# Feed-forward input products with 512 moving columns, and weights laid out in order of use

## What is computed

```python
def conv_glu_ffn(h, w_in, conv_w, conv_b, w_out):
    a, b = jnp.split(h @ w_in, 2, axis=-1)
    taps = conv_w[:, None, :]
    a = lax.conv_general_dilated(a, taps, ...) + conv_b      # depthwise, causal, 3 taps
    return (jax.nn.silu(a) * b) @ w_out

def _swiglu(h, w_in, w_out):
    gate, up = jnp.split(h @ w_in, 2, axis=-1)
    return (jax.nn.silu(gate) * up) @ w_out
```

## Time and profile before

| | |
|---|---|
| median of 3 runs | 2264.7 us |
| the profiled execution | 2262.3 us, its span 2260.5 us |
| TensorE matmuls / weight loads | 2098.9 us (93%) / 1978.4 us (88%), 15863 each |
| DVE, ACT, POOL busy | 1170.3, 981.6, 546.8 us |
| granted TensorE clock | 0.938 of full on average |
| chain that ended last | TensorE 82%, DVE 10%, ACT 5% |
| HBM | 142 GB/s over the span |

### The profile page before, as it was taken

How to read it: one execution, slowest core, us unless ns; L and a number is a source line. 1 busy time by engine, 2 the same in 40 slices (tenths; PEclk the granted TensorE clock), 3 DMA queues, 4 the chain that set the end, 5 groups by cost and what they waited for, 6 DMA issues and landing times.

```text
span 2260.5 us, 36891 instructions
## 1 busy us (share of the span) xinstructions
PE 2098.9 (93%) x15863; PEld 1978.4 (88%) x15863; DVE 1170.3 (52%) x1402; ACT 981.6 (43%) x1144; POOL 546.8 (24%) x153
## 2 busy tenths in 40 slices
PE   6988999969999997999976999999999989899999
PEld 5975799968789997999976899989999989669999
DVE  4335466755556766445786644334444432765433
ACT  3323344443444434434624444357434447544433
POOL 1100012221112231322142122453022256211232
PEclk8966799989999998999988999999999999899999
DMA  9400144535224553555521265535555535523653
GB/s 224 154 25 0 57 149 168 178 124 164 98 96 166 187 191 102 189 184 163 184 94 56 95 204 184 169 117 171 185 164 190 183 125 160 140 65 114 204 168 111
DMA packets 265345, 322.17 MB, mean 143 GB/s; under 512 B 15837, under 2 KB 245076, under 8 KB 264980
## 3 DMA queue, kind: packets, MB, share of 16 engines
q1 hardware_dynamic: 252692, 304.49, 41.1%
q0 software_dynamic: 2816, 9.44, 1.7%
q10 hardware_dynamic: 9728, 6.67, 1.4%
HBM read 319.45 MB, written 1.12 MB: 142 GB/s over the span
## 4 chain that ended last, share of the span: by engine, by line
PE 82%; DVE 10%; ACT 5%; issue 1%; ACTq 1%; DMA 1%; POOL 1%; SPq 0%; DVEq 0%
PE bank L370 23%; PE bank L371 22%; PE bank L372 22%; DVE lo L343 3%; PE bank L411 2%; PE bank L430 2%; ACT hi L337 1%; PE bank L433 1%; PE bank L413 1%; PE bank L446 1%; PE bank L1624 1%; ACT arena L1566 1%; PE bank L1405 1%; DVE arena L1480 1%; DVE xl L754 1%
## 5 line engine op out<-in xcount | busy, mean ns | idle before, releaser
L370 PE MATMUL bank<-xh,hi 128*128 128x256 f32 x3208 | 931.0, 290 | 55.5 <-DVE xl L754 22.9
L371 PE MATMUL bank<-xl,hi 128*128 128x256 f32 x3208 | 917.1, 286 | 0.0
L372 PE MATMUL bank<-xh,lo 128*128 128x256 f32 x3208 | 916.3, 286 | 0.0
L343 POOL TENSOR_TENSOR lo<-ring,hi 128x2048 fp32r<-128x2048 f32 x100 | 472.6, 4729 | 1470.9 <-ACT hi L337 1470.9
L337 ACT ACTIVATE hi<-ring 128x2048 fp32r<-128x2048 f32 x291 | 550.5, 1899 | 482.0 <-PE bank L372 465.3
L343 DVE TENSOR_TENSOR lo<-ring,hi 128x2048 fp32r<-128x2048 f32 (+1 forms) x191 | 502.8, 2633 | 410.7 <-ACT hi L337 410.5
L370 PEld LDWEIGHTS bank<-xh,hi 128*128 128x128 f32 x3208 | 624.7, 195 | 69.3 <-issue 38.1
L371 PEld LDWEIGHTS bank<-xl,hi 128*128 128x128 f32 x3208 | 625.0, 195 | 4.9 <-issue 4.8
L372 PEld LDWEIGHTS bank<-xh,lo 128*128 128x128 f32 x3208 | 624.6, 195 | 0.2
L370 PE MATMUL bank<-gg,hi 128*128 128x256 f32 x1056 | 303.9, 288 | 20.2 <-DVE gg L695 20.2
L371 PE MATMUL bank<-gg,hi 128*128 128x256 f32 x1056 | 303.1, 287 | 0.0
(11 more groups left out here) (234 smaller groups left out, 2041.9 us busy)
## 6 DMA issues: line engine op xcount, KB each, us to landing
ring<-in_ffn_w_in SPq DMA_DIRECT2D x132, 1024.0 KB, 5.1
ring<-in_ffn_w_out SPq DMA_DIRECT2D x66, 1024.0 KB, 4.9
ring<-in_w_kv SPq DMA_DIRECT2D x24, 1024.0 KB, 5.2
ring<-in_a_w_in SPq DMA_DIRECT2D x16, 1024.0 KB, 5.5
ring<-in_od_w_in SPq DMA_DIRECT2D x12, 1024.0 KB, 6.5
ring<-in_b_w_q SPq DMA_DIRECT2D x12, 1024.0 KB, 5.1
ring<-in_ev_w_in SPq DMA_DIRECT2D x11, 1024.0 KB, 5.2
arena<-rel_rows POOLq DMA_DIRECT2D x16, 384.0 KB, 3.8
```

Of the source, the lines that this page charges most:

```text
L343: ns.tensor_tensor(lo[n % RING][:, 0:w], ring[n % RING][:, 0:w], hi[n % RING][:, 0:w].bitcast(F32), ALU.subtract).then_inc(lo_ok[lo_by[n]], 1)
L370: nc.tensor.matmul(out_, lh, rh, start=start, stop=False, **kw)
L371: nc.tensor.matmul(out_, lh, rl, start=False, stop=False, **kw)
L372: return nc.tensor.matmul(out_, ll, rh, start=False, stop=stop, **kw)
```

## The change

- The high and low activations come to lie side by side, so that one matmul has both as 512 moving columns, with the high weights loaded once. Its two halves of 256 columns fall into the two halves of a whole PSUM bank; the low weights' product (256 columns) is added to the first half. The 96 matmuls and weight loads of an `ff_in` become 64.
- A chunk of `w_in` now holds 128 columns of the gate and the 128 of the up half that belong to them; a chunk is one half e of the step. Each half takes two whole banks, so a step takes all of banks 0 to 3, and the half e of `ff_in` waits until that half of step j-1 has been read.
- Per half, ACT copies the second halves of two banks out of PSUM (`ff_x`), DVE adds them to the first halves (`ff_m`), and then multiplies by `rs_b` in SBUF.
- All weight arrays are laid out ahead in order of use, so that a chunk is 128 rows of 8 KB in one piece, and the compression weights come in two DMAs instead of four.
- The semaphores of the softmax parts are shared between the mixers; their counts and waits stay what they were.

```diff
-        xh = sb("xh", [P, KT, T], F32R)
-        xl = sb("xl", [P, KT, T], F32R)
+        xx = sb("xx", [P, KT, 2, T], F32R)
+        xh, xl = xx[:, :, 0, :], xx[:, :, 1, :]
...
-        def ff_in(pe, j, par, n, F, first, it=None):
-
-            if first is None:
-                pe.wait_ge(ff_read, 2 * (F + j))
-            for h in range(2):
-                wait_split(pe, n + h, it)
-                wh, wl = slot(n + h, of=hi), slot(n + h, of=lo)
-                B = bank[2 * par + h]
-                for e in range(2):
-                    ee = slice(e * P, (e + 1) * P)
+        def ff_in(pe, j, n, F, first, it=None):
+
+            for e in range(2):
+                if first is None:
+                    pe.wait_ge(ff_read, 2 * (F + j) + (e + 1))
+                wait_split(pe, n + e, it)
+                wh, wl = slot(n + e, of=hi), slot(n + e, of=lo)
+                for h in range(2):
+                    B, hh = bank[2 * e + h], slice(h * P, (h + 1) * P)
                     for k in range(KT):
-                        if first is not None and h == 0 and e == 0 and k % 2 == 0:
+                        if first is not None and e == 0 and h == 0 and k % 2 == 0:
                             pe.wait_ge(xg_new, first + k // 2 + 1)
-                        last = product(B[:, e * T:(e + 1) * T], wh[:, k, ee], wl[:, k, ee], xh[:, k, :], xl[:, k, :],
-                                       k == 0, k == KT - 1)
+                        both = xx[:, k, :, :].rearrange("p s t -> p (s t)")
+                        nc.tensor.matmul(B[:, :], wh[:, k, hh], both, start=k == 0, stop=False)
+                        last = nc.tensor.matmul(B[:, 0:T], wl[:, k, hh], xh[:, k, :], start=False, stop=k == KT - 1)
                 last.then_inc(chunk_mul, 1)
...
-            dve.wait_ge(chunk_mul, c_of)
-            ga = bank[2 * par][:, :].rearrange("p (e t) -> p e t", e=2)
-            ub = bank[2 * par + 1][:, :].rearrange("p (e t) -> p e t", e=2)
-            dst = ff_a[:, par, :, 2:2 + T] if conv is not None else ff_c[:, par, :, :]
-            nc.vector.tensor_tensor(dst, ga, rs2, ALU.mult).then_inc(ff_read, 1)
-            nc.vector.tensor_tensor(ff_b[:, par, :, :], ub, rs2, ALU.mult).then_inc(ff_read, 1)
+            for e in range(2):
+                dve.wait_ge(chunk_mul, c_of + (e - 1))
+                m2, two = ff_m[:, par, e, :, :], banks[:, 2 * e:2 * e + 2, :]
+                dve.wait_ge(ff_cross, 2 * (F + j) + (e + 1))
+                nc.vector.tensor_tensor(m2, two[:, :, 0:T], ff_x[:, e, :, :], ALU.add).then_inc(ff_read, 1)
+                dve.wait_ge(ff_read, 2 * (F + j) + (e + 3))
+                if conv is not None:
+                    nc.vector.tensor_tensor(ff_a[:, par, e, 2:2 + T], m2[:, 0, :], rs_b[:, :], ALU.mult)
+                    nc.vector.tensor_tensor(m2[:, 1, :], m2[:, 1, :], rs_b[:, :], ALU.mult).then_inc(ff_scaled, 1)
+                else:
+                    nc.vector.tensor_tensor(m2, m2, rs2, ALU.mult).then_inc(ff_scaled, 1)
...
-            if it is None:
-                hi_until(act, m + 4)
-            else:
-                for c in (m + 3, m + 4):
-                    split_hi(act, c, it)
+            for e in range(2):
+                if it is None:
+                    hi_until(act, m + 2)
+                act.wait_ge(chunk_mul, chunk_of_step(b, j, first) + (e - 1))
+                nc.scalar.activation(ff_x[:, e, :, :], banks[:, 2 * e:2 * e + 2, T:2 * T], ACT.Copy).then_inc(ff_cross, 1)
+                if it is None:
+                    hi_until(act, m + 3 + e)
+                else:
+                    split_hi(act, m + 3 + e, it)
             if conv is None:
-                act.wait_ge(ff_read, 2 * (F + j) + 3)
-                nc.scalar.activation(ff_s[:, par, :, :], ff_c[:, par, :, :], ACT.Silu).then_inc(ff_silu, 1)
+                act.wait_ge(ff_scaled, 2 * (F + j) + 2)
+                nc.scalar.activation(ff_s[:, par, :, :], ff_m[:, par, :, 0, :], ACT.Silu).then_inc(ff_silu, 1)
...
-                for i, w in enumerate(("cmp_w_k", "cmp_w_v")):
-                    src = A[w].rearrange("(l d) e -> d l e", d=DH)
-                    for hf in range(2):
-                        act.dma_start(CW_[hf * DH:(hf + 1) * DH, i, :].rearrange("p (l e) -> p l e", e=DH),
-                                      src).then_inc(cmp_in, 16)
+                for i in range(2):
+                    act.dma_start(CW_[:, i, :], A["cmp_w"][i]).then_inc(cmp_in, 16)
...
-            def load_cols(n, w, c0, width, it=None):
+            def load(n, w, c, it=None):
                 free(n, it)
-                src = w.rearrange("(k p) n -> p k n", p=P)
-                sp.dma_start(slot(n, width), src[:, :, bass.ds(c0, width)] if it is not None
-                             else src[:, :, c0:c0 + width]).then_inc(chunk_in[n % RING], 16)
+                src = w[bass.ds(c * P, P), :] if it is not None else w[c * P:(c + 1) * P, :]
+                sp.dma_start(ring[n % RING][:, :], src).then_inc(chunk_in[n % RING], 16)
```

More of the change, by code:

```diff
@@ L165, in build @@
         ident = sb("ident", [P, P])
-        bank = [ctx.enter_context(nc.psum_tensor(f"bank{i}", [P, 512], F32)) for i in range(8)]
+        banks = ctx.enter_context(nc.psum_tensor("banks", [P, 8, 512], F32))
+        bank = [banks[:, i, :] for i in range(8)]
         arena = sb("arena", [P, ARENA])
@@ L237, in build @@
         W = {
-            "ev_in": A["ev_w_in"], "ev_out": A["ev_w_out"], "od_in": A["od_w_in"], "od_out": A["od_w_out"],
-            "hg_in": A["a_w_in_2"], "hg_out": A["a_w_out_2"], "kv": A["w_kv_2"], "dq": A["b_w_q_2"],
-            "do": A["b_w_o_2"],
-        }
[L242 to L246, removed]
+            w: A[w] for w in ("ev_in", "ev_out", "od_in", "od_out", "hg_in", "hg_out", "kv", "dq", "do")
+        }
+        ffn_in, ffn_out = {}, {}
+        for i, b in enumerate(("conv0", "conv1", "glu0", "glu1", "glu2", "glu3")):
+            ffn_in[b], ffn_out[b] = A["ffn_in"][i], A["ffn_out"][i]
         streams = {
@@ L372, in product @@
             return nc.tensor.matmul(out_, ll, rh, start=False, stop=stop, **kw)
+        soft_sem = {k: sem("soft_" + k) for k in ("qk", "masked", "max", "exp", "rec", "p", "turned", "pt", "pv", "oh", "o")}
+        soft_total = dict.fromkeys(soft_sem, 0)
         class Soft:
@@ L383, in __init__, with at @@
                 self.before = {"pe": {}, "dve": {}, "act": {}}
[L384 to L394, removed]
+                pairs, n_sub = len(units) // (2 if units[0]["last"] else 4), len(units) * ns
+                gates = sum(un.get("gate") is not None for un in units)
+                adds = {"qk": n_sub, "masked": n_sub, "max": len(units), "exp": len(units), "rec": len(units) + gates,
+                        "p": len(units), "turned": n_sub, "pt": n_sub, "pv": n_sub, "oh": pairs - len(held), "o": pairs}
+                self.base = {k: soft_total[k] for k in adds}
+                for k, n in adds.items():
+                    soft_total[k] += n
+            def at(self, k, n):
+                return soft_sem[k], self.base[k] + n
         def soft_pe(pe, s):
@@ L413, in pv @@
                 nc.tensor.matmul(ob[pb:pb + DH, P:T], sub["v"][1], q[:, T:384], start=False,
-                                 stop=un["last"] and g == ns - 1, skip_group_check=True).then_inc(s.pv, 1)
+                                 stop=un["last"] and g == ns - 1, skip_group_check=True).then_inc(soft_sem["pv"], 1)
             for i in range(U + s.lag):
@@ L631, in pe_ffn @@
             F, n = info[b]["ff0"], info[b]["c0"]
-            ff_in(pe, 0, 0, n, F, first_xg(b))
+            ff_in(pe, 0, n, F, first_xg(b))
             if info[b]["prep"]["kind"] != "regain":
@@ L1863, in _ @@
                     wi, wo = ffn_in[b], ffn_out[b]
-                    load_cols(n, wi, 0, CW)
-                    load_cols(n + 1, wi, DFF, CW)
+                    load(n, wi, 0)
+                    load(n + 1, wi, 1)
                     def turn(i, m0, it):
```

133 lines of the change are left out of this document (76 added, 57 removed).

## The result

The changed kernel takes **2295.98 us** (median of four runs, 2294.0 to 2299.98) against 2264.76: ratio 1.0135, interval 1.0112 to 1.0159. It is slower by 1.35%, outside the range that was given (2226 to 2290). Its profiled execution, the slowest of the four, spans 2297.8 us, 37.3 more than before.

The account below looks back on a forecast made before the run. TensorE (93% busy) was taken as the bound, with conv's closed DVE, ACT and POOL chain only 0.11 us under it. Conv +34, glu -20, first mixer -8 made +6 on 2262.3: 2268.3, median about 2270, range 2226 to 2290.

Parts of the forecast that it names:

- The pair: FFN input products: a 512- plus a 256-column matmul takes 0.340 us against 0.360 for three, saving 0.64 us per step.
- The third rival: FFN input products: columns decide, the pair takes 0.360 us as three did, about 2300 us in all; chance 0.11.
- the point of decision: FFN input products: a pair of about 0.345 us, where the slower rival's whole passes 0.3%.
- Conv: Conv FFNs: closed chain of POOL, DVE and ACT lengthens from 17.17 to 18.8 us per step; +17 per FFN, +34 for two.
- Start waits: Start of the five FFNs with statistics: step 1 waits for step 0's first addition, 2.2 us each.
- First mixer: First mixer: two compression-weight DMAs free ACT earlier and end TensorE's 6.34 us wait; -8 us with the clock.
- Elsewhere 0: Outside the other terms: 8 KB chunk pieces taken as 0 (-4 to +1), shared semaphores as 0.
- my case: Whole kernel: the main forecast, 2252 to 2286 us with conv 26 to 48 and pair 0.333 to 0.346; chance 0.60.

Follow-up runs that it names:

- x2_wide_only: Changed kernel with the low-weight products of the FFN input side left out, so only 512-column matmuls follow each other there; 2205.2 us (one run).
- x3_grouped: Changed kernel with each bank's eight 512-column matmuls first, then its eight 256-column ones, instead of in turns; 2298.5 us, ratio to before 1.0137.
- x4_half_pool: Changed kernel with POOL's low part of the output weights only half as wide in the FFNs, the rest left out; 2252.9 us (one run).
- x6_add_first: Changed kernel with step 0's cross copies ahead of ACT's square root and its additions ahead of DVE's reciprocals in five FFNs; 2287.2 us, ratio to before 1.0086.
- x1_layout: Changed kernel's weight layout and first-mixer DMAs only, with the products, banks and DVE operations of the kernel before; 2259.14 us, ratio to before 0.9964.
- x8_pool_later: `x1_layout` plus one wait: in the first mixer POOL's low part of chunk 14 follows DVE's fourth addition; 2252.46 us, ratio to before 0.9937.
- after: The changed kernel itself, against the kernel before; 2295.98 us, ratio 1.0135.
- x7_hybrid: Changed kernel with old products in conv FFNs; glu FFNs have pairs grouped eight wide, eight narrow, and additions ahead of reciprocals; 2256.34 us, ratio to before 0.9953.
- x9_all: `x7_hybrid` with the first-mixer POOL wait of `x8_pool_later` added; 2250.24 us, ratio to before 0.9928.

## Why the prediction was wrong

The whole was 31 us too low on the profiled executions (+6 forecast, +37.3 measured), 26 by the medians. It is right in its mechanism for conv and for the start waits, wrong in the size of one term, what a pair saves, and that term is some 19 of the 31 us (44 glu steps, 0.43 us each).

- **The pair: the step that failed.** "I take 0.220 ... plus 0.12 for the other: 0.340" measures 0.353. The 0.220 was set beside the 0.216 of bf16 rows with one weight row. In fp32r with 128 weight columns `x2_wide_only` measures 0.2276: fitted to that and to 0.120, each matmul has a constant of 0.012, and one of three saved is 0.012, not the 0.020 I took. Of the 13 ns by which the pair is dearer than forecast, 8 are the wide matmul (0.2276 for 0.220), and 4 or 5 are the turns between lengths (`x3_grouped`). Forty glu steps behind the clearing save 0.21 us each instead of 0.64: 17 us of the 22 missing in the glu stages, and the four step 0s have 2 more. The prediction named a pair outside 0.33 to 0.35 as a sign that it is wrong, and 0.353 is outside.
- **The third rival,** columns decide, has the sign right. The measured 0.353 lies between my 0.340 and its 0.360, on its side of the 0.345 that the text gave as the point of decision, and the time, 2296, is near its 2300. Its chance of 0.11 was too little. That point was itself wrong: by the prediction's own sum (1.4 us for each ns of the pair) the whole passes 0.3% already at 0.341. The Trainium skill (TensorE: Matmul & The Clock Gate, on the back-to-back gap) had pointed that way, with some 2.5 ns for each matmul above the columns; the runs show 13 and 14 ns above the columns at 2.4 GHz and a pair that saves 7, neither that nor my 20.
- **Conv: mechanism right, and the total partly by luck.** Chain period 18.8 forecast, 18.67 measured; the wait for POOL's low part 2.2 forecast, 1.6 measured, as the pairs save less. `x2_wide_only` and `x4_half_pool` show the cause. A conv FFN was forecast at +17 and measured +18.8 and +17.3, but its terms miss in both directions: nine periods give 12 instead of 13.7, the starts +2.0 each against 0.9, the ends +4.7 and +3.3 against 2.2.
- **Start waits: place and length right, price too low.** The wait is 2.27 us against 2.2, and the price of the low clock behind it was left out in glu, though the earlier trace rows had shown it (7.22 us for 47 distances of 0.12, so 1.6 us, not the 1.4 that the prediction read): the starts of glu0, glu1 and glu3 take 3.5, 3.6 and 3.6 us more. Some 5 us of the glu error. `x6_add_first` takes both away, save for its own wait of 1.11 us in two of them.
- **First mixer: right to its own end, then half given back.** The wait was gone and 7.6 us gained; 4.2 of them fell to a collision of DVE and POOL, a term that the prediction didn't have, and that the profile before missed by 0.13 us. `x1_layout` has it too, and `x8_pool_later` takes it away. I had asked what comes late next on TensorE there, and not what POOL's next start would meet.
- **Elsewhere 0:** the stretches between FFNs moved by +1.6, -0.1, +1.0, -3.0 and +0.5 us. The largest, between glu1 and glu2, takes 174.0, 174.1 and 176.3 us in `after`, `x6_add_first` and `x4_half_pool`, which don't differ there, so it is not told from none.
- **The range:** the upper bounds of my case, conv 48 and a pair of 0.346, add up to 2270 + 14 + 8 = 2292, not 2286. The range ended below my own bounds, and the measured time lies above both.

## What to carry to other kernels

Price a matmul from rows of its own type, its own number of weight columns and its own length, and where one is missing, measure it first: here one matmul of three saved was worth 7 ns in turn and 11 grouped, not 20. Where DVE, ACT and POOL form a chain that closes on itself and sets the step, what is gained on TensorE doesn't count and what DVE gets is added nearly in full (1.59 us more on DVE, 1.50 on the chain's period); a change of this kind belongs in the stages whose chain has room. Read for each stage that starts earlier what POOL and DVE will then meet: one wait on POOL took 4.2 us out of its stage (6.7 between the medians), and the pairs in glu with the reordered starts 2.8 between the medians (2259.14 and 2256.34), with intervals that overlap.

## What the runs showed of the hardware

- In fp32r with 128 weight columns 256 moving columns take 0.120 us and 512 take 0.2276; with 16 weight columns 0.113 and 0.2317. The shorter load is cheaper with the one and dearer with the other, so the constant of 12 ns, a fit to two lengths, is not simply the time of a load and doesn't hold for 16 columns. What it is stays open.
- A shift of 0.13 us decides a block of 4.2 us. When POOL's low part starts 0.16 us ahead of DVE's fourth addition, which has two inputs in SBUF, that addition takes some 4.7 us (6.16 less three times 0.48), so in `after` and in seven of the ten runs; in the kernel before it takes 0.55, and POOL's takes 4.88 instead of 4.54. The Trainium skill (SBUF — State Buffer, on the shared port pair) says that a GpSimd operation and a DVE operation with two SBUF inputs exclude each other, and that whichever starts first holds the pair for its whole length. The rows agree that one waits for the other; but in the kernel before POOL's recorded start, 112.384, is 0.014 us ahead of the fourth addition's, 112.398, and DVE went through, so starts this close don't tell who comes first.
- A wait of 2.3 us at a glu FFN's start costs 3.5 to 3.6 where it takes TensorE's granted clock from 1.00 to 0.65 (a mean of its two levels, 2.4 and 1.2 GHz). The wait of 1.11 us at the start of glu1 costs 1.1 in `x7_hybrid`, where the clock stays at 1.00, and 2.3 in `x9_all`, where it is 0.87 over the next input products (both against `x1_layout`). And the same step 0 of glu1, in `x9_all` and in `x7_hybrid`, takes a microsecond more when the clock is granted later:

```profile
1269.60:1281.80 12.20, 12.04 (x64) 9.65 (x65) 7.43 (x11) 5.85 (x10) 0.00 (x0) 1.00 0.32 116
...
1273.80:1287.00 13.20, 13.16 (x64) 10.76 (x65) 7.52 (x11) 5.85 (x10) 0.00 (x0) 0.87 0.27 101
```

Both have 64 matmuls; the clock (third column from the right) is 1.00 in the first and 0.87 in the second. An experiment on a start shouldn't be judged by one execution.
